# ScalarE's order in a softmax stage: the exponentials of one unit against the high half of another's probabilities

## The chip, the cores and the metric

One core of one Trainium2 chip runs the whole program. The metric is the device time of one execution in microseconds (us), as a median of several runs.

## What is computed

Two layers over 2048 tokens of width 1024. The first is sliding-window attention with 16 heads of 64 in 4 key/value groups and a sink per head; the second a pooling mixer. The change touches the attention's softmax. Cut from the reference:

```python
scores = jnp.einsum('bnqkgd,bnskd->bnkgqs', qb, kb).astype(jnp.float32) * (HEAD_DIM ** -0.5)
...
m = jnp.maximum(jnp.max(scores, axis=-1, keepdims=True), sink)
p = jnp.exp(scores - m)
denom = jnp.sum(p, axis=-1, keepdims=True) + jnp.exp(sink - m)
probs = (p / denom).astype(v.dtype)
o = jnp.einsum('bnkgqs,bnskd->bnqkgd', probs, vb)
...
return (o * jax.nn.silu(g)) @ w_out
```

## The kernel before

The program has four stages in a row on each engine: queries, keys and values (`qkv_stage`), gates (`gate_stage`), attention with its output projection (`attend_stage`), and the pooling layer (`pool_stage`). To keep float32 precision at the speed of the faster format, every operand of a large matmul is split into a high and a low half (ScalarE rounds to the high half, VectorE subtracts it from the value to get the low one), and three products are added up.

`attend_stage` works in 64 **units**: a unit is a block of 128 tokens by one key/value group, that is 4 heads. Nothing is scheduled by a tool: each engine has a hand-written loop over **slots** i = 0 to 67, and in slot i it does its piece of several units at once, in a fixed order. Engines wait for each other by semaphores, and each engine takes its instructions strictly in order. In slot i the pieces are:

- TensorE: scores of unit i (L1371); the first half of a weight fold (L1432) or of an output projection (L1415); the transposes of unit i-1's probabilities into the one buffer `tr` (L1381); the second half of fold or projection; the values of unit i-2 (L1399).
- ScalarE (`scalar`): the high half of z of unit i-3 (`z_hi`, L1207); the copy of the scores against the previous key block (`previous`, L1183); the high half of the transposed probabilities of unit i-1 (`p_hi`, L1198, into `ph`); the four exponentials of unit i with their sums (`exps`, L1191, into `pr` and `den`); in the first slots the high half of fold weights (`fold_high`, L1224 and L1227) and the eviction of a fold (`fold_evict`, L1232); in later slots, every second one, a square (L1214, L1217).
- VectorE (`vector`): the gating of unit i-3 (`gated`, L1289, into `z`); reciprocal and multiply of unit i-1 (`divide`, L1273, L1275); the predicated copy and maximum of unit i (`scores`, L1265, L1269); the low half of z (`z_lo`, L1296); every second slot a residual (L1304); the low half of unit i-1's probabilities (`p_lo`, L1281, into `pl`); in the first slots the low half of fold weights (`fold_low`, L1311 and L1313).
- GpSimd: four masks of unit i-1, two from `ph` and two from `pl`, into `pt` (L1147); every second slot the addition of a square (L1156).

A **fold** multiplies two weight matrices of the pooling layer ahead of time; there are 16, their weights are split in slots 0 to 15 and every fourth of these slots (0, 4, 8, 12) also splits a second weight. Output projections fill TensorE's slots from 19 on. The waits that matter here: `exps(u)` waits for the maximum of u (`max_done`), `p_hi(u)` for the transposes of u (`ptr_done`), `p_lo(u)` for `p_hi(u)` (`ph_done`), `previous(u)` for the scores (`s_done`), `z_hi(u)` for the gating (`z_done`), the transposes of u for the multiply of u (`prob_done`) and for `p_lo(u-1)` (`pl_done`), and the values of u for its four masks (`pt_done`).

Of the kernel before, what the change touches and what calls it, by code (L numbers as in the profile page):

```python
# [25 lines left out]
def wait(eng, sem, count):  # L26
    if count > 0:
        eng.wait_ge(sem, count)
# [931 lines left out]
def attend_stage(nc, sem_of, dims, weights, qk, ga, xt_d, sinks_d, wvt, w_group, qt_d, kt_d, vs_d, sg_d, wo_d, wp_d, x1t_d, ident,  # L960
# [8 lines left out]
    UNITS = NB * KV  # L969
# [56 lines left out]
    def chunks_ended(i):  # L1026
        return [c for c in range(CHUNKS - KC) if first_slot(c) + HALVES == i]

    def place(m):
        cur, prev = m % 3, (m - 1) % 3  # L1030
        return min(cur, prev), max(cur, prev), 0 if cur < prev else 1
# [141 lines left out]
    def scalar(act, next_hi):  # L1173
        def previous(u):
            m, g = u // KV, u % KV
            act.wait_ge(s_done, u + 1)
            wait(act, exp_done, u - 3)
            src = s_ps[:, u % 2, :, 1 - place(m)[2], :]
            if m == 0:
                act.wait_ge(consts_set, 5)  # L1180
                nc.scalar.activation(sc[:, g, :, 0:P], src, ACT.Identity, bias=first[:, :]).then_inc(prev_done, 1)
            else:
                nc.scalar.activation(sc[:, g, :, 0:P], src, ACT.Copy).then_inc(prev_done, 1)  # L1183

        def exps(u):
            g = u % KV
            act.wait_ge(max_done, u + 1)
            wait(act, ptr_done, u - 1)
            wait(act, rden_done, u - 1)
            for h in range(GROUP):  # L1190
                last = nc.scalar.activation(pr[:, u % 2, h, :], sc[:, g, h, :], ACT.Exp, bias=neg_max[:, u % 2, h:h + 1],  # L1191
                                            accum_out=den[:, u % 2, h:h + 1])
            last.then_inc(exp_done, 1)

        def p_hi(u):
            act.wait_ge(ptr_done, u + 1)
            wait(act, pt_done, 4 * u - 2)
            nc.scalar.activation(ph[:, :].bitcast(F32R), tr[:, :], ACT.Copy).then_inc(ph_done, 1)  # L1198

        def z_hi(u):  # L1200
            m, g = u // KV, u % KV
            s, t = m // PER, m % PER
            act.wait_ge(z_done, u + 1)
            wait(act, y_done, KC * (s - 1))
            if u == LAP:
                act.wait_ge(fold_done, FOLDS)
            nc.scalar.activation(zt[:, s % 2, HI, 2 * g:2 * g + 2, t * P:(t + 1) * P], z[:, u % 2], ACT.Copy).then_inc(zhi_done, 1)  # L1207

        def square(c):
            act.wait_ge(x1_done, c + 1)  # L1210
            s, d = c // KC, c % KC
            if d == 0:
                wait(act, st_done, s)
                nc.scalar.activation(acc[:, :], x_t[:, c % 3, :], ACT.Square).then_inc(sqx_done, 1)  # L1214
            else:
                wait(act, acc_done, (KC - 1) * s + (d - 2 if d >= 3 else 0))
                nc.scalar.activation(sqx[:, c % 2], x_t[:, c % 3, :], ACT.Square).then_inc(sqx_done, 1)  # L1217

        def fold_high(u):
            f = u // PAIRS  # L1220
            if u % PAIRS == 0:
                act.wait_ge(wg_loaded[f % 2], 16 * (f // 2 + 1))
                wait(act, fold_done, PAIRS * (f - 1))
                nc.scalar.activation(wg[:, f % 2, HI], wg_raw[:, f % 2], ACT.Copy).then_inc(wg_hi, 1)  # L1224
            act.wait_ge(fold_loaded[u % 3], 16 * (u // 3 + 1))
            wait(act, fold_done, u - 2)
            nc.scalar.activation(wv[:, u % 3, HI], wv_raw[:, u % 3], ACT.Copy).then_inc(fold_hi, 1)  # L1227

        def fold_evict(u):
            act.wait_ge(fold_done, u + 1)  # L1230
            wait(act, fold_stored[u % 2], 16 * GC * (u // 2))
            nc.scalar.activation(folded[:, u % 2].rearrange("p c k n -> p k c n"), fold_ps[:, u % 2], ACT.Copy).then_inc(fold_out, 1)  # L1232

        for i in range(LAST + 1):
            if 0 <= i - BEHIND < UNITS:
                z_hi(i - BEHIND)
            if i < UNITS:
                previous(i)
            if 1 <= i <= UNITS:
                p_hi(i - 1)  # L1240
            if i < UNITS:
                exps(i)
            if i < FOLDS:
                fold_high(i)
            if 0 <= i - 3 < FOLDS:
                fold_evict(i - 3)
            for c in chunks_ended(i):
                square(c)
        for c in range(CHUNKS - KC, CHUNKS):
            next_hi(act, c - CHUNKS + KC)  # L1250
            square(c)
# [219 lines left out]
    def last_rstd(pool):  # L1471
        rstd(pool, NSB - 1)

    return {"sync": sync, "gpsimd": gpsimd, "scalar": scalar, "vector": vector, "tensor": tensor, "first_load": first_load,
            "last_sum": last_sum, "last_mean": last_mean, "last_rstd": last_rstd, "chunks": CHUNKS, "units": UNITS, "s_done": s_done,
            "pt_done": pt_done, "o_done": o_done, "y_done": y_done, "ptr_done": ptr_done, "exp_done": exp_done, "cur_done": cur_done,
# [460 lines left out]
```

## Time and profile before

| | us |
|---|---|
| median of 3 runs | 1541.5 (1540.37 to 1541.74) |
| the profiled execution, its own time | 1541.43 |
| its span | 1539.7 |
| TensorE matmuls busy | 1438.1 (93% of the span) |
| VectorE busy | 895.0 (58%) |
| ScalarE busy | 542.1 (35%) |
| GpSimd busy | 385.7 (25%) |
| mean granted TensorE clock | 0.987 of full speed |

The span reaches from the first to the last recorded instruction; the time also holds what lies around it. A share is a mean over four stages: the stage of the change lies between 578.7 and about 946 us. In a timeline row the first number is the start from the span's start, the second the duration, and the brackets tell how long the engine idled just before and what ended the wait.

### The profile page before, as it was taken

The numbers are of one execution on the slowest core, as the hardware profiler recorded it, in microseconds if no ns is written. First come the engines' busy times: TensorE is split into PE (matmuls) and PEld (weight loads), VectorE is DVE, ScalarE is ACT, GpSimd is POOL, SyncE is SP. The second block draws the span as 40 slices with busy tenths as digits, with TensorE's granted clock in tenths as the row PEclk, the third lists the DMA queues.
The fourth block names the chain that finished last, engine by engine and source line by source line (L and its number), as shares of the span: only waits on it lengthen the run. The fifth ranks groups of instructions, "written<-read, shape, count | busy, mean of one in ns | idle before, by whom it ended". The sixth has DMA issues, their size and how long they took to land.

```text
span 1539.7 us, 20207 instructions
## 1 busy us (share of the span) xinstructions
PE 1438.1 (93%) x7240; PEld 1211.1 (79%) x7240; DVE 895.0 (58%) x1524; ACT 542.1 (35%) x1270; POOL 385.7 (25%) x551
## 2 busy tenths in 40 slices
PE   2789999999889996789999999899999999999999
PEld 1677777788678786778888888688888888888887
DVE  7766667665444446887777775535456452645522
ACT  2433334433211116775666564322222222222200
POOL 2333333321222213454555555220000000000000
PEclk9999999999989998999999999999999999999999
DMA  8644555534987786756767765941111552112142
GB/s 315 226 144 168 196 196 192 193 118 169 336 313 293 259 310 220 254 213 257 262 251 277 271 242 196 328 130 41 55 42 62 171 191 76 42 55 74 50 150 82
DMA packets 96787, 285.62 MB, mean 186 GB/s; under 512 B 10768, under 2 KB 40496, under 8 KB 87088
## 3 DMA queue, kind: packets, MB, share of 16 engines
q1 hardware_dynamic: 87760, 250.74, 45.3%
q0 software_dynamic: 8928, 33.59, 6.3%
q8 instruction: 58, 0.95, 0.2%
q14 instruction: 41, 0.34, 0.1%
HBM read 196.22 MB, written 88.08 MB: 185 GB/s over the span
## 4 chain that ended last, share of the span: by engine, by line
PE 58%; DMA 4%; DVE 4%; ACT 3%; issue 2%; POOL 0%; ACTq 0%; SPq 0%; DVEq 0%; POOLq 0%
PE po_f_ps L1843 23%; PE po_y_ps L1859 11%; PE at_y_ps L1415 9%; PE ga_g_ps L933 5%; PE at_o_ps L1399 5%; PE at_s_ps L1371 3%; PE at_tr L1381 2%; DMA ga_ada<-in_ada_w 2%; ACT at_pr L1191 1%; DMA x_mid_t<-at_x 1%; DMA po_xn<-x_mid_t 1%; DVE at_sc L1265 1%; DMA silu_gates_t<-ga_sg 1%; DVE at_neg_max L1269 1%; DVE at_z L1289 0%
## 5 line engine op out<-in xcount | busy, mean ns | idle before, releaser
L1843 PE MATMUL po_f_ps<-po_ht,po_w 128*128 128x512 f32 x1536 | 348.9, 389 | 0.0
L1843 PEld LDWEIGHTS po_f_ps<-po_ht,po_w 128*128 128x128 f32 x1536 | 288.1, 188 | 60.1 <-DVE po_ht L1705 0.3
L667 PE MATMUL qk_proj<-qk_w_qkv,qk_ht 128*128 128x512 f32 x1152 | 282.6, 401 | 12.7 <-DVE qk_ht L460 6.7
L667 PEld LDWEIGHTS qk_proj<-qk_w_qkv,qk_ht 128*128 128x128 f32 x1152 | 217.1, 192 | 59.9 <-DVE qk_ht L460 8.0
L1415 PE MATMUL at_y_ps<-at_zt,at_w 128*128 128x512 f32 x768 | 198.6, 400 | 5.8 <-DVE at_x L1304 5.2
L1859 PE MATMUL po_y_ps<-po_zt,po_w 128*128 128x512 f32 x768 | 174.7, 389 | 0.0
L1859 PEld LDWEIGHTS po_y_ps<-po_zt,po_w 128*128 128x128 f32 x768 | 144.1, 188 | 29.9
L1415 PEld LDWEIGHTS at_y_ps<-at_zt,at_w 128*128 128x128 f32 x768 | 138.4, 190 | 31.6 <-issue 7.1
L1692 DVE TENSOR_TENSOR po_w<-po_raw,po_w 128x1024 fp32r<-128x1024 f32 x48 | 58.8, 1225 | 129.1 <-ACT po_w L1626 129.1
L1147 POOL TENSOR_SCALAR_AFFINE_SELECT at_pt<-at_ph 128x512 fp32r<-128x512 f32 x128 | 83.6, 677 | 187.2 <-ACT at_ph L1198 187.2
L306 POOL TENSOR_TENSOR qk_rq<-qk_mq,qk_half 128x8 f32<-128x8 f32 (+1 forms) x48 | 70.2, 1462 | 189.4 <-DVE qk_mq L487 189.4
L1191 ACT ACTIVATE at_pr<-at_sc,at_neg_max 128x129 f32<-128x129 f32 x256 | 99.7, 393 | 7.2 <-DVE at_neg_max L1269 5.9
L1399 PE MATMUL at_o_ps<-at_pt,at_vs 128*128 128x256 f32 x744 | 100.6, 285 | 0.0
L1399 PEld LDWEIGHTS at_o_ps<-at_pt,at_vs 128*128 128x128 f32 x744 | 97.5, 192 | 3.8
L1626 ACT ACTIVATE po_w<-po_raw 128x1024 fp32r<-128x1024 f32 x48 | 50.6, 1054 | 108.4 <-PE po_y_ps L1859 108.4
L1551 POOL DMA_DIRECT2D po_xn<-x_mid_t x32 | 17.4, 544 | 262.7 <-DVE po_ht L1705 256.7
L1773 DVE SCALAR_TENSOR_TENSOR po_x<-po_y_ps,mod,po_x 128x512 f32<-128x512 f32 x32 | 24.0, 751 | 99.7 <-PE po_y_ps L1859 99.7
L1147 POOL TENSOR_SCALAR_AFFINE_SELECT at_pt<-at_pl 128x512 fp32r<-128x512 f32 x128 | 79.2, 641 | 3.2 <-DVE at_pl L1281 2.3
L1371 PE MATMUL at_s_ps<-at_kt,at_qt 128*128 128x256 f32 x512 | 73.0, 286 | 0.0
L872 ACT ACTIVATE ga_sg<-ga_g_ps 128x512 f32<-128x512 f32 x32 | 18.9, 595 | 142.7 <-PE ga_g_ps L933 113.9
L933 PE MATMUL ga_g_ps<-ga_x,ga_w_late 128*128 128x512 f32 x288 | 68.6, 398 | 0.0
L1371 PEld LDWEIGHTS at_s_ps<-at_kt,at_qt 128*128 128x128 f32 x512 | 67.3, 195 | 0.1
(168 smaller groups left out, 1985.8 us busy)
## 6 DMA issues: line engine op xcount, KB each, us to landing
at_w<-out_weight_split SPq DMA_DIRECT2D x32, 1024.0 KB, 6.6
queries_t<-qk_late SPq DMA_DIRECT2D x16, 1024.0 KB, 4.3
ga_ada<-in_ada_w POOLq DMA_DIRECT2D x64, 256.0 KB, 4.6
at_qt<-queries_t SPq DMA_DIRECT2D x16, 1024.0 KB, 8.2
ht_split<-qk_ht SPq DMA_DIRECT2D x6, 2048.0 KB, 9.6
values_split<-qk_late SPq DMA_DIRECT2D x16, 768.0 KB, 5.0
at_vs<-values_split SPq DMA_DIRECT2D x16, 768.0 KB, 5.0
qk_late<-in_ada_w SPq DMA_DIRECT2D x16, 512.0 KB, 5.6
```

The costliest lines, as they stand in the source:

```text
L306: nc.gpsimd.tensor_tensor(rq[:, heads], mq[:, heads], half[:, heads], ALU.pow).then_inc(rq_done, 1)
L667: last = nc.tensor.matmul(proj[:, b * BANK:(b + 1) * BANK], ht[:, s % 2, m, k, t * P:(t + 1) * P], w_qkv[:, w, k, b * BANK:(b + 1) * BANK] ...
L933: last = nc.tensor.matmul(g_bank(q), split_of(f, w)[:, k * P:(k + 1) * P], h, start=(i == 0), stop=(i == 3 * KC - 1))
L1147: nc.gpsimd.affine_select(out=pt[:, u % 2, kind, :].rearrange("p (h t) -> p h t", h=GROUP), in_=(ph if hi else pl)[:, :].rearrange("p (h t ...
L1191: last = nc.scalar.activation(pr[:, u % 2, h, :], sc[:, g, h, :], ACT.Exp, bias=neg_max[:, u % 2, h:h + 1], accum_out=den[:, u % 2, h:h + 1])
L1371: last = nc.tensor.matmul(s_ps[:, u % 2, h, :, :], qt[:, m % 2, GROUP * g + h, :], kt[:, low:high + 1:high - low, g, part, :], start=(part ...
L1399: last = nc.tensor.matmul(o_ps[:, 0:2 * P], v, moving[:, :, parity, :], start=(i == 0), stop=(i == 6 * len(parts) - 1))
L1415: last = nc.tensor.matmul(y_ps[:, c % 2, :], w[:, c % 3, a, k, :], zt[:, s % 2, b, k, :], start=(k == 0 and (a, b) == PRODUCTS[0]), stop=( ...
L1626: nc.scalar.activation(w[:, i % 2, HI].rearrange("p k c -> p (k c)"), raw[:, (RING0 + i) % RAW].rearrange("p k c -> p (k c)"), ACT.Copy).t ...
L1692: nc.vector.tensor_tensor(w[:, i % 2, LO].rearrange("p k c -> p (k c)"), raw[:, (RING0 + i) % RAW].rearrange("p k c -> p (k c)"), w[:, i % ...
L1843: last = nc.tensor.matmul(f_ps[:, bank(j, h), :], w[:, i % 2, a, k, :], ht[:, h, m, k, :], start=(n == 0), stop=(n == 3 * KC - 1))
L1859: last = nc.tensor.matmul(y_ps[:, h, :], w[:, i % 2, a, k, :], zt[:, h, m, k, :], start=(n == 0), stop=(n == 3 * KC - 1))
```

## The change

In each slot ScalarE takes `exps(i)` right after `previous(i)`, and `p_hi(i-1)` after it. No instruction, buffer or wait is added or removed; the other engines' programs are the same.

```diff
@@ -1236,10 +1236,9 @@
                 z_hi(i - BEHIND)
             if i < UNITS:
                 previous(i)
+                exps(i)
             if 1 <= i <= UNITS:
                 p_hi(i - 1)
-            if i < UNITS:
-                exps(i)
             if i < FOLDS:
                 fold_high(i)
             if 0 <= i - 3 < FOLDS:
```

ScalarE, one slot with a fold, before. L1207 is the high half of z, L1183 the copy of scores, L1198 the high half of the probabilities, L1191 the exponentials, L1227 the high half of the fold weights, L1232 the fold's eviction:

```order
L1207 ACTIVATE at_zt<-at_z 128x2x128
L1183 ACTIVATE at_sc<-at_s_ps 128x4x128
L1198 ACTIVATE at_ph<-at_tr 128x512
L1191 ACTIVATE at_pr,at_den<-at_sc,at_neg_max 128x129 x4
L1227 ACTIVATE at_early_wv<-at_early_wv_raw 128x512
L1232 ACTIVATE at_folded<-at_y_ps 128x2x2x128
```

The same slot with the change:

```order
L1207 ACTIVATE at_zt<-at_z 128x2x128
L1183 ACTIVATE at_sc<-at_s_ps 128x4x128
L1191 ACTIVATE at_pr,at_den<-at_sc,at_neg_max 128x129 x4
L1198 ACTIVATE at_ph<-at_tr 128x512
L1227 ACTIVATE at_early_wv<-at_early_wv_raw 128x512
L1232 ACTIVATE at_folded<-at_y_ps 128x2x2x128
```

The high half moves behind the four exponentials and stays ahead of the fold's two instructions. VectorE's order in such a slot is the same before and after; it ends with the low half of the probabilities (L1281) and of the fold weights (L1313), and the next slot begins with the gating (L1289):

```order
L1265 COPY_PREDICATED at_sc<-at_keep_cur,at_s_ps 128x4x128 [waits at_prev_done]
L1269 TENSOR_REDUCE at_neg_max<-at_sc 128x4 [waits at_exp_done,at_cur_done]
L1296 TENSOR_TENSOR at_zt<-at_z,at_zt 128x2x128 [waits at_zhi_done]
L1281 TENSOR_TENSOR at_pl<-at_tr,at_ph 128x512 [waits at_pt_done,at_ph_done]
L1313 TENSOR_TENSOR at_early_wv<-at_early_wv_raw,at_early_wv 128x512 [waits at_fold_hi]
L1289 SCALAR_TENSOR_TENSOR at_z<-at_o_ps,at_sg 128x256 [waits at_zlo_done,at_o_done]
L1273 RECIPROCAL at_rden<-at_den 128x4 [waits at_exp_done]
L1275 TENSOR_TENSOR at_pr<-at_pr,at_rden 128x4x128 [waits at_rden_done]
```

Nothing moved here; L1281 waits for the high half that now comes later.

## Rows read from the trace of the kernel before

**Rows 1.** The page, its first line.
```profile
span 1539.7 us, 20207 instructions
```

**Rows 2.** Windows: us, then busy us of each engine, TensorE clock, DMA share, GB/s.
```profile
602.00:680.00 78.00, 60.91 (x456) 56.24 (x456) 63.28 (x109) 54.95 (x172) 33.32 (x52) 0.98 0.69 241
609.00:613.50 4.50, 3.86 (x21) 3.66 (x20) 3.58 (x8) 2.93 (x11) 1.36 (x3) 0.62 0.91 310
680.00:689.00 9.00, 7.82 (x63) 7.24 (x61) 7.52 (x15) 7.11 (x25) 5.76 (x9) 1.00 0.74 280
770.00:860.00 90.00, 90.00 (x580) 79.96 (x578) 67.25 (x120) 55.03 (x184) 49.57 (x72) 1.00 0.69 259
```

**Rows 3.** Timeline of one fold slot: start us, us, engine, line, operation, idle before.
```profile
623.78 0.41 ACT L1191 ACTIVATE at_pr<-at_sc,at_neg_max 128x129 f32<-128x129 f32 x1 [0.31 <-DVE at_neg_max L1269]
...
625.34 0.62 ACT L1227 ACTIVATE at_early_wv<-at_early_wv_raw 128x512 fp32r<-128x512 f32 x1
...
625.99 0.89 DVE L1313 TENSOR_TENSOR at_early_wv<-at_early_wv_raw,at_early_wv 128x512 fp32r<-128x512 f32 x1 [0.94 <-ACT at_early_wv L1227]
...
626.80 0.41 DVE L1289 SCALAR_TENSOR_TENSOR at_z<-at_o_ps,at_sg 128x256 f32<-128x256 f32 x1
...
627.24 0.42 ACT L1207 ACTIVATE at_zt<-at_z 128x256 fp32r<-128x256 f32 x1 [0.81 <-DVE at_z L1289]
...
627.57 0.58 ACT L1183 ACTIVATE at_sc<-at_s_ps 128x512 f32<-128x512 f32 x1
...
628.18 0.74 DVE L1265 COPY_PREDICATED at_sc<-at_keep_cur,at_s_ps 128x512 f32<-128x512 uint32 x1 [0.16 <-ACT at_sc L1183]
...
628.95 0.69 DVE L1269 TENSOR_REDUCE at_neg_max<-at_sc 128x4 f32<-128x516 f32 x1
...
629.68 0.41 ACT L1191 ACTIVATE at_pr<-at_sc,at_neg_max 128x129 f32<-128x129 f32 x1 [0.31 <-DVE at_neg_max L1269]
```

**Rows 4.** Timeline, TensorE, the same slot.
```profile
626.58 0.94 PE L1432 MATMUL at_y_ps<-at_early_wg,at_early_wv 128*128 128x256 f32 x6 [0.64 <-ACT at_folded L1232]
628.08 0.66 PE L1381 MATMUL at_tr<-ident,at_pr 128*128 128x128 f32 x4 [0.56 <-DVE at_pr L1275]
```

**Rows 5.** Timeline, high half, low half, masks and gating in later slots.
```profile
687.29 0.68 DVE L1281 TENSOR_TENSOR at_pl<-at_tr,at_ph 128x512 f32<-128x512 f32 x1
...
687.89 0.41 DVE L1289 SCALAR_TENSOR_TENSOR at_z<-at_o_ps,at_sg 128x256 f32<-128x256 f32 x1
...
708.22 0.60 ACT L1198 ACTIVATE at_ph<-at_tr 128x512 fp32r<-128x512 f32 x1 [1.23 <-PE at_tr L1381]
...
708.85 0.69 DVE L1281 TENSOR_TENSOR at_pl<-at_tr,at_ph 128x512 f32<-128x512 f32 x1
708.88 1.22 POOL L1147 TENSOR_SCALAR_AFFINE_SELECT at_pt<-at_ph 128x512 fp32r<-128x512 f32 x2 [3.11 <-ACT at_ph L1198]
```

**Rows 6.** Timeline, ScalarE, first exponential of units 1, 16, 19 and 63.
```profile
588.37 0.39 ACT L1191 ACTIVATE at_pr<-at_sc,at_neg_max 128x129 f32<-128x129 f32 x1
...
678.11 0.41 ACT L1191 ACTIVATE at_pr<-at_sc,at_neg_max 128x129 f32<-128x129 f32 x1 [0.31 <-DVE at_neg_max L1269]
...
691.91 0.40 ACT L1191 ACTIVATE at_pr<-at_sc,at_neg_max 128x129 f32<-128x129 f32 x1
...
942.15 0.39 ACT L1191 ACTIVATE at_pr<-at_sc,at_neg_max 128x129 f32<-128x129 f32 x1
```

**Rows 7.** Timeline, TensorE, scores of two neighbouring slots with output projection.
```profile
705.23 1.12 PE L1371 MATMUL at_s_ps<-at_kt,at_qt 128*128 128x256 f32 x8
...
710.82 1.12 PE L1371 MATMUL at_s_ps<-at_kt,at_qt 128*128 128x256 f32 x8
```

**Rows 8.** Timeline, a GpSimd addition and the VectorE multiply beside it.
```profile
899.53 1.29 POOL L1156 TENSOR_TENSOR at_acc<-at_acc,at_sqx 128x512 f32<-128x512 f32 x1
...
899.77 1.60 DVE L1275 TENSOR_TENSOR at_pr<-at_pr,at_rden 128x512 f32<-128x512 f32 x1
```

**Rows 9.** Timeline, TensorE, the transposes of the last unit.
```profile
946.68 0.65 PE L1381 MATMUL at_tr<-ident,at_pr 128*128 128x128 f32 x4 [0.85 <-DVE at_pr L1275]
```

## Prediction

> **What bounds the kernel now.** The windows come first, because the change touches one stage only, from 578.7 to about 946 us of a span of 1539.7 us [rows 1], and that stage has three stretches with different limits. From 602 to 680 us TensorE is busy for 60.9 of 78.0 us, and no other engine is full either (VectorE 63.3, ScalarE 55.0, GpSimd 33.3): a stretch in which nobody is full is bounded by a loop of waits [rows 2]. From 680 to 689 us the slots have neither a weight fold nor an output projection. From 689 us on TensorE is busy all the time, 90.0 of 90.0 us between 770 and 860 [rows 2]: there TensorE sets the pace.
>
> The timeline of one slot of the first stretch shows the loop [rows 3]. From one unit's first exponential (623.78) it is 1.56 us until ScalarE is free for the high half of the fold weights (625.34), 0.65 until VectorE takes their low half (625.99), 0.81 until the gating behind it (626.80), 0.44 to the split of z on ScalarE (627.24), 0.33 to the copy of the previous scores (627.57), 0.61 to the predicated copy (628.18), 0.77 to the maximum (628.95) and 0.73 to the next unit's first exponential (629.68). The sum is 5.90 us, the whole slot. The high half of the probabilities, which the change moves, is on none of these steps. TensorE idles twice in that slot, 0.64 and 0.56 us [rows 4].
>
> In the third stretch two neighbouring slots begin 5.59 us apart (705.23 and 710.82) [rows 7]. Over all of it, from unit 19 (691.91) to unit 63 (942.15), 44 slots take 250.24 us, 5.69 each [rows 6].
>
> **The change, part by part.** No instruction is added or removed. Each of 64 high halves on ScalarE now stands behind four exponentials of the unit ahead, not before them. It can start no earlier than 1.56 us after the first exponential.
>
> *What is queued behind it.* VectorE's low half waits for the high half and starts 0.63 us after it (708.22 to 708.85) [rows 5]. Behind the low half, in VectorE's order, stand in a fold slot the low half of the fold weights, and then in every slot the next gating, which follows a low half after 0.60 us (687.29 to 687.89) [rows 5]. ScalarE's split of z waits for that gating, and behind the split stands the next copy of scores, which leads to the next exponentials. So a new loop is closed, one turn per slot: exponentials 1.56, high half to low half 0.63, low half to gating 0.60, then the known links 0.44 + 0.33 + 0.61 + 0.77 + 0.73. That is **5.67 us** in a slot without a fold. With a fold VectorE has one more operation of 0.60 between low half and gating, and the slot takes **6.27 us**. The second operand of that operation is no longer late: ScalarE makes it right behind the high half.
>
> *Fold slots, units 1 to 16.* 15 intervals, 89.74 us now (588.37 to 678.11) [rows 6]. Each grows by 6.27 - 5.90 = 0.37 at least. It can grow more, because the split of the fold weights now falls among GpSimd's masks, which start 0.66 us after the high half and run for 1.22 [rows 5]. What such a meeting costs is shown by a multiply that was asked for at 899.77 beside an addition on GpSimd running from 899.53 to 900.82: it ended at 901.37, 0.55 after the addition [rows 8]. The split would be asked for at 0.63 + 0.60 = 1.23 after the high half, at the joint between the first mask and the second (0.66 + 0.61 = 1.27). If it gets the joint it loses almost nothing, if not, about 0.5. I take 0.45 for the interval, near the lower end, since the margin is on its side: 15 x 0.45 = 6.8. Three of these slots begin a new weight group and have two splits in a row, the second certain to meet a mask: 3 x 0.4 = 1.2. Together **+8.0**; the ends are 15 x 0.37 = 5.6 and 15 x 0.9 = 13.5.
>
> A rule bears on this. The Trainium skill, "SBUF — State Buffer", Terms, says that VectorE and GpSimd take the port pair they share as an exclusive lock for a full instruction and that the loser blocks. The multiply above agrees. By that rule alone, with no look at the joint, every split would lose and the sum would be that of the first rival.
>
> *Units 16 to 19.* Three intervals take 13.80 us now (678.11 to 691.91) [rows 6]; at 5.67 each they take 17.0: **+3.2**. This is the surest term: TensorE has nothing here that would hide it.
>
> *Units 19 to 63.* The loop of 5.67 is longer than TensorE's 5.59, but the stretch now averages 5.69, since a part of its slots is lengthened, among others by meetings as in rows 8. 44 x 5.67 = 249.5 against 250.24: **-0.7**. TensorE cannot go under 44 x 5.59 = 246.0, which bounds a gain at 4.2; at 5.72 a slot the loss is 1.4.
>
> *Ends.* At unit 1 the exponentials no longer stand behind a high half: about -0.3. At unit 63, from the first exponential to the transposes it is 4.53 now (942.15 to 946.68) [rows 6, 9]; on the new path 1.56 + 0.63 + 0.60 and, from gating to transposes, 1.28 (626.80 to 628.08) [rows 3, 4], 4.07: **-0.5**. At a start of this size neither is more than a correction.
>
> *Costed at nothing.* GpSimd's four masks come later by the same 1.8 us as the high half, but TensorE needs them one slot later; in a slot with output projection about 1 us is left. The squares and fold evictions on ScalarE stand behind the high half too; they end 1.1 to 1.6 after it starts, and the gating's result is there only after 0.63 + 0.60 + 0.44 = 1.67. If that cover went, the split of z would wait for them. DMA issues stay in their order, on SP's queue. What comes after 946 us is bounded by TensorE and by data of this stage, so a delay passes through in full.
>
> The sum: 8.0 + 3.2 - 0.7 - 0.3 - 0.5 = **+9.7 us**. The profiled execution took 1541.43 us, its span 1539.7, and the median of the three runs is 1541.5, so both bases give the same: **1551.2 us**. About 0.2% (3 us) is what a measurement of this kernel can tell from no change.
>
> **The rivals.**
>
> *Lock lost at the joint.* The split of the fold weights comes a few hundredths later than 1.23 and finds the second mask running, to 1.88. Then it ends 0.55 after it, 0.5 later than assumed, in 15 slots: +7.5, **1558.7 us**. For it: a margin of 0.04 us. Against it: an operation already waiting when a mask ends should go first. If the multiply, asked for about 0.5 after the gating, loses its joint too (1.77 against the mask's end at 1.88), the predicated copy is some 0.4 later in the 44 slots as well: +17 more, 1576.
>
> *The idle time absorbs it (the other side).* ScalarE has 0.81 us idle before the split of z and VectorE 0.94 before the fold's low half [rows 3], more than the 0.50 and 0.60 that move there. If both moved operations fitted, first exponential to gating would stay 3.02 (623.78 to 626.80), the first two stretches would keep their times, and the third would run between 5.59 and 5.67: -0.7 to -4.2, about **1539 us**. It decides at 3.02: the new sequence is 1.56 + 0.63 + 0.60 + 0.60 = 3.39. It would need the low half not to hold up VectorE's next operation, and the in-order rows speak against that.
>
> *No effect.* The high half ends up at its old time because something else, already there, holds the exponentials as long: 1541.4. The 0.31 us idle ahead of the exponentials is a wait for the maximum [rows 3], so nothing of the kind is seen.
>
> *Clock.* Once in the first stretch, between 609.0 and 613.5 us, after a slot with two long waits, the granted clock was 0.62 of full speed [rows 2], a mix of the two levels of 1.2 and 2.4 GHz. Longer fold slots idle TensorE more. A drop of that length costs 0.38 x 4.5 = 1.7 us of work, against the slot's idle time of 0.64 + 0.56, which grows by 0.37: 0.1 us each, and perhaps 1 us where the third stretch starts. Five drops: about 1553. The Trainium skill, "TensorE: Matmul & The Clock Gate", Part 1, makes an idle engine fall to the half rate; by it the fold slots would fall oftener, and the time is this rival's.
>
> **How the numbers follow.** Forecast 0.64; lock lost 0.22 (0.04 of it in both places); no effect 0.06; absorbed 0.04; clock 0.04. The range holds the forecast's own bounds, 8.0 replaced by 5.6 and a third stretch at -2, to the lock lost with 2 us more: **1547 to 1561**. Left out are the two cases without a loss (0.10), the double loss (0.04) and a remainder. Slower 0.64 + 0.22 + 0.04 = 0.90, same 0.06, faster 0.04.
>
> **What would show it.** Fold slots near 6.3 us from first exponential to first exponential, 5.67 for units 16 to 19 and again near 5.7 from 19 to 63; the idle time before the fold's low half gone, and the low half of the probabilities directly before it; TensorE idle before the transposes in the third stretch, by under 0.1 us a slot. A fold's low half of 1.1 us or more would be the first rival. Wrong I would be if the fold slots stayed at 5.9, or if the third stretch left 5.6 to 5.75.

## The result, and the profile after

| | before | with the change |
|---|---|---|
| median | 1541.62 us (4 runs, 1540.37 to 1542.31) | 1555.06 us (4 runs, 1553.16 to 1556.96) |
| ratio | | 1.0089, 95% interval 1.0077 to 1.0102 |
| the profiled execution, its own time | 1541.43 | 1556.96 |
| mean granted TensorE clock | 0.987 | 0.981 |

The change costs 13.4 us. It was forecast to cost 9.7, within 1547 to 1561.

The first line of the page after stands against [rows 1]; the profiled execution was the slowest of its four, so its span is 15.5 us longer, 2 more than the medians differ.

```profile
span 1555.2 us, 20207 instructions
```

To see where the 15.5 us are, the first exponential of each unit is read from the ScalarE timeline of both kernels. The intervals between them add up to this (positions in us from the span's start; units 1, 16, 19 and 63 of before are [rows 6]):

| stretch | before | after | difference | forecast |
|---|---|---|---|---|
| start of the program to unit 0 | 582.36 | 583.16 | +0.8 | 0 |
| unit 0 to 1 | 6.01 | 5.72 | -0.3 | -0.3 |
| units 1 to 16 (fold slots) | 89.74 | 100.10 | +10.4 | +8.0 |
| units 16 to 19 | 13.80 | 17.01 | +3.2 | +3.2 |
| units 19 to 63 | 250.24 | 251.37 | +1.1 | -0.7 |
| unit 63 to the end of the span | 597.55 | 597.84 | +0.3 | -0.5 |

The windows after, with the same columns as [rows 2]:

```profile
602.00:690.00 88.00, 64.72 (x455) 60.35 (x454) 62.48 (x107) 54.38 (x175) 43.92 (x52) 0.92 0.62 211
690.00:700.00 10.00, 6.92 (x53) 6.13 (x52) 6.53 (x13) 6.02 (x20) 5.77 (x8) 0.97 0.74 274
700.00:860.00 160.00, 159.71 (x1015) 142.00 (x1016) 115.73 (x212) 92.57 (x323) 94.94 (x124) 0.99 0.68 255
```

TensorE is still busy nearly all the time in the last of them (159.71 of 160.00), but it gets less done: 1015 matmuls, against 1025 in the same window of the kernel before. In that kernel VectorE's gating waited for TensorE's values in 42 of the 44 slots recorded between 700 and 945 us; in the changed kernel only the two slots that hold the sums of squares wait for them. The stretch is no longer TensorE's: one slot there shows the ring of the prediction, link by link. The timeline of ScalarE and VectorE, units 22 and 23:

```profile
723.03 0.40 ACT L1191 ACTIVATE at_pr<-at_sc,at_neg_max 128x129 f32<-128x129 f32 x1 [1.55 <-DVE at_neg_max L1268]
...
724.59 0.58 ACT L1198 ACTIVATE at_ph<-at_tr 128x512 fp32r<-128x512 f32 x1
...
725.20 0.69 DVE L1280 TENSOR_TENSOR at_pl<-at_tr,at_ph 128x512 f32<-128x512 f32 x1 [1.87 <-ACT at_ph L1198]
...
725.81 0.41 DVE L1288 SCALAR_TENSOR_TENSOR at_z<-at_o_ps,at_sg 128x256 f32<-128x256 f32 x1
...
726.25 0.42 ACT L1207 ACTIVATE at_zt<-at_z 128x256 fp32r<-128x256 f32 x1 [1.09 <-DVE at_z L1288]
...
726.58 0.58 ACT L1183 ACTIVATE at_sc<-at_s_ps 128x512 f32<-128x512 f32 x1
...
727.19 0.75 DVE L1264 COPY_PREDICATED at_sc<-at_keep_cur,at_s_ps 128x512 f32<-128x512 uint32 x1 [0.16 <-ACT at_sc L1183]
...
727.97 0.69 DVE L1268 TENSOR_REDUCE at_neg_max<-at_sc 128x4 f32<-128x516 f32 x1
...
728.70 0.41 ACT L1191 ACTIVATE at_pr<-at_sc,at_neg_max 128x129 f32<-128x129 f32 x1 [1.54 <-DVE at_neg_max L1268]
```

First exponential 723.03, high half 724.59 (+1.56), low half 725.20 (+0.61), gating 725.81 (+0.61), split of z 726.25 (+0.44), copy 726.58 (+0.33), predicated copy 727.19 (+0.61), maximum 727.97 (+0.78), next first exponential 728.70 (+0.73): 5.67 us. Of the 44 intervals from unit 19 to 63, 42 lie between 5.66 and 5.70. Before, they alternated between about 5.43 and 5.88 in most of the stretch, and VectorE's multiply met GpSimd's addition of a square, as in [rows 8], in 18 of the 43 slots between 697 and 940 us (1.59 to 1.62 us instead of 0.69). In the changed kernel 42 of the 43 multiplies take 0.69: the masks come later, the addition stands behind them, and so it no longer runs beside the multiply. The change thus closes a ring in this stretch and takes meetings out of it, and the two nearly cancel. The exponentials now wait for the maximum (1.54 us in the slot shown), and VectorE's low half waits for the high half; the same operation had no such wait in [rows 5].

A fold slot after, which stands against [rows 3]:

```profile
623.40 0.58 ACT L1198 ACTIVATE at_ph<-at_tr 128x512 fp32r<-128x512 f32 x1
...
624.01 0.69 DVE L1280 TENSOR_TENSOR at_pl<-at_tr,at_ph 128x512 f32<-128x512 f32 x1 [1.87 <-ACT at_ph L1198]
...
624.04 1.75 POOL L1147 TENSOR_SCALAR_AFFINE_SELECT at_pt<-at_ph 128x512 fp32r<-128x512 f32 x2 [3.12 <-ACT at_ph L1198]
...
624.62 0.68 DVE L1312 TENSOR_TENSOR at_early_wv<-at_early_wv_raw,at_early_wv 128x512 fp32r<-128x512 f32 x1
...
625.22 0.42 DVE L1288 SCALAR_TENSOR_TENSOR at_z<-at_o_ps,at_sg 128x256 f32<-128x256 f32 x1
...
625.67 0.42 ACT L1207 ACTIVATE at_zt<-at_z 128x256 fp32r<-128x256 f32 x1 [0.69 <-DVE at_z L1288]
...
625.75 1.18 DVE L1274 TENSOR_TENSOR at_pr<-at_pr,at_rden 128x512 f32<-128x512 f32 x1
...
625.75 1.67 POOL L1147 TENSOR_SCALAR_AFFINE_SELECT at_pt<-at_pl 128x512 fp32r<-128x512 f32 x2
...
626.85 0.74 DVE L1264 COPY_PREDICATED at_sc<-at_keep_cur,at_s_ps 128x512 f32<-128x512 uint32 x1
...
628.35 0.41 ACT L1191 ACTIVATE at_pr<-at_sc,at_neg_max 128x129 f32<-128x129 f32 x1 [1.78 <-DVE at_neg_max L1268]
```

Two things are to be seen here. The split of the fold weights on VectorE (624.62) got its turn at the joint of two masks, as forecast: it took 0.68 us, no more. But GpSimd paid for it. Its first pair of masks, 1.22 us in [rows 5], takes 1.75 here and ends at 625.79, and VectorE's multiply is asked for at 625.75, just as a mask of the next pair takes over. The multiply lasts 1.18 us. The predicated copy, which follows in VectorE's order, starts at 626.85, 1.63 behind the gating instead of 1.38 in [rows 3]. So the slot, from the first exponential at 621.84 to the next at 628.35, takes 6.51 us and not 6.27. In the three slots with a new weight group the second split takes 1.12 us instead of 0.68 besides, and they take 7.54.

### The profile page after: what moved, and what is told of

Its sections match the earlier page's. It is cut to its first block, busy times and chain, and to the rows that moved or that the text cites. A ratio compares the mean times of both kernels' runs of the same rounds, so it can differ in the third digit from the quotient of the medians.

```text
span 1555.2 us, 20207 instructions
## 1 busy us (share of the span) xinstructions
PE 1444.4 (93%) x7240; PEld 1217.1 (78%) x7240; DVE 891.7 (57%) x1524; ACT 533.8 (34%) x1270; POOL 415.8 (27%) x551
## 4 chain that ended last, share of the span: by engine, by line
PE 56%; DVE 12%; issue 10%; DMA 8%; ACT 7%; POOL 6%; SPq 1%; POOLq 0%; ACTq 0%; DVEq 0%
PE po_f_ps L1842 22%; PE po_y_ps L1858 11%; PE qk_proj L667 9%; PE ga_g_ps L933 6%; POOL at_pt L1147 3%; PE at_y_ps L1414 3%; DMA ga_ada<-in_ada_w 3%; ACT at_pr L1191 3%; DMA po_xn<-x_mid_t 1%; PE at_o_ps L1398 1%; DVE at_sc L1264 1%; DVE at_neg_max L1268 1%; POOL at_acc L1156 1%; DMA ga_raw<-in_attn_w_gate 1%; POOL qk_rq L306 1%
## 5 line engine op out<-in xcount | busy, mean ns | idle before, releaser
L1191 ACT ACTIVATE at_pr<-at_sc,at_neg_max 128x129 f32<-128x129 f32 x256 | 100.0, 392 | 104.3 <-DVE at_neg_max L1268 104.3
L1147 POOL TENSOR_SCALAR_AFFINE_SELECT at_pt<-at_pl 128x512 fp32r<-128x512 f32 x128 | 107.8, 864 | 0.0
L1398 PEld LDWEIGHTS at_o_ps<-at_pt,at_vs 128*128 128x128 f32 x744 | 101.9, 201 | 4.5 <-issue 0.7
L1398 PE MATMUL at_o_ps<-at_pt,at_vs 128*128 128x256 f32 x744 | 104.9, 292 | 0.5 <-issue 0.5
L1280 DVE TENSOR_TENSOR at_pl<-at_tr,at_ph 128x512 f32<-128x512 f32 x64 | 44.3, 692 | 92.8 <-ACT at_ph L1198 92.8
```

The lines of the kernel that those rows point to most:

```text
L1147: nc.gpsimd.affine_select(out=pt[:, u % 2, kind, :].rearrange("p (h t) -> p h t", h=GROUP), in_=(ph if hi else pl)[:, :].rearrange("p (h t ...
L1398: last = nc.tensor.matmul(o_ps[:, 0:2 * P], v, moving[:, :, parity, :], start=(i == 0), stop=(i == 6 * len(parts) - 1))
```

## The experiments

Two theories stand against each other. **The ring**: the delayed high half closes a loop through the in-order queues of ScalarE and VectorE, and its price in a stretch is the loop's length less what bounded the stretch before. **A price per slot**: each of 64 high halves is late, and everything behind it is late by the same 0.21 us. Beside them, for the fold slots, the port of VectorE and GpSimd against TensorE's clock.

### The change in some slots only

The changed order in slots 16 to 63 alone, shown against the changed kernel:

```diff
             if i < UNITS:
                 previous(i)
+            if FOLDS <= i < UNITS:
                 exps(i)
             if 1 <= i <= UNITS:
                 p_hi(i - 1)
             if i < FOLDS:
+                exps(i)
+            if i < FOLDS:
                 fold_high(i)
```

> The changed order only in slots 16 to 63; in slots 0 to 15 the high half stands ahead of the exponentials as in the kernel before. Theory of the loop (the delay is that of the closed ring high half, low half, gating, copy, maximum, exponentials, and its price depends on what else stands on that ring): units 1 to 16 back to 89.7 us from first exponential to first exponential, 16 to 19 at 17.0, 19 to 63 at 251.4; that is 4.3 us more than the kernel before, 1546 us. Rival, a price per slot whatever stands in it (64 delayed high halves, 13.4 us, 0.21 each): 48 of 64 slots, 10 us more, 1552.

Measured: 1544.77 us, ratio to the kernel before 1.0026 (1.0014 to 1.0037), which is 4.0 us more. Units 1 to 16 took 90.3, 16 to 19 17.00, 19 to 63 251.5.

The other half, with the changed order in slots 0 to 15 and the old one from 16 on, again against the changed kernel:

```diff
             if i < UNITS:
                 previous(i)
+            if i < FOLDS:
                 exps(i)
             if 1 <= i <= UNITS:
                 p_hi(i - 1)
+            if FOLDS <= i < UNITS:
+                exps(i)
```

> The changed order only in slots 0 to 15. Theory of the loop: units 1 to 16 take 100.1 us as in the changed kernel (ordinary intervals 6.51, those of a new weight group 7.54), 16 to 19 13.8 and 19 to 63 250.2 as in the kernel before: 10.4 - 0.3 = 10.1 more, 1551.7 us. Rival, a price per slot: 16 of 64 slots, 3.4 more, 1545. Added to the other half's loss the two should give the whole loss of 13.4, if nothing is shared between the stretches.

Measured: 1551.9 us, ratio 1.0066 (1.0053 to 1.0078), 10.2 more. Units 1 to 16 took 100.04, 16 to 19 13.93, 19 to 63 250.21. A quarter of the slots carries three quarters of the loss; a price per slot would have put 3.4 us here and 10 in the other half. The two parts make 14.2, the whole 13.7 by its ratio. Each of these figures is uncertain by about 2 us, so no sharing between the stretches is to be seen, and the intervals in the traces agree: each stretch is as in the kernel whose order it has, within 0.6 us.

### A link taken out of the ring

In the changed kernel ScalarE copies the previous scores first and splits z after that, so the copy no longer waits for the gating:

```diff
         for i in range(LAST + 1):
+            if i < UNITS:
+                previous(i)
             if 0 <= i - BEHIND < UNITS:
                 z_hi(i - BEHIND)
             if i < UNITS:
-                previous(i)
                 exps(i)
```

> The changed kernel, with ScalarE's copy of the previous scores ahead of the split of z, so that the copy no longer waits for the gating. Theory of the loop: the predicated copy then waits for the multiply alone, 0.54 + 0.60 = 1.14 behind the gating instead of 1.39: units 16 to 19 5.42 each, 16.3 instead of 17.0; 19 to 63 bounded by TensorE again, 5.59 to 5.65 a slot, 246.5 to 249 instead of 251.4; the fold slots unchanged at 6.51, since there the multiply is already what the predicated copy waits for. Total 1550 to 1552. Rival, the split of z is not on the ring (ScalarE is simply late by the moved order): no interval changes, 1555.

Measured: 1550.4 us, ratio 1.0060 (1.0048 to 1.0073). Units 16 to 19 took 5.42, 5.42 and 5.41, 16.25 in all; 19 to 63 took 248.1; units 1 to 16 99.9. All as the ring has it: the fold slots did not move, as said, and the other two stretches did. A slot between 16 and 19, ScalarE and VectorE:

```profile
692.09 0.58 ACT L1183 ACTIVATE at_sc<-at_s_ps 128x512 f32<-128x512 f32 x1
...
692.35 0.41 DVE L1289 SCALAR_TENSOR_TENSOR at_z<-at_o_ps,at_sg 128x256 f32<-128x256 f32 x1
...
692.80 0.42 ACT L1207 ACTIVATE at_zt<-at_z 128x256 fp32r<-128x256 f32 x1
...
692.88 0.69 DVE L1275 TENSOR_TENSOR at_pr<-at_pr,at_rden 128x512 f32<-128x512 f32 x1
...
693.49 0.74 DVE L1265 COPY_PREDICATED at_sc<-at_keep_cur,at_s_ps 128x512 f32<-128x512 uint32 x1
```

The copy (692.09) stands ahead of the gating (692.35), and the predicated copy follows the multiply at once: 693.49 - 692.35 = 1.14. The split of z is on the ring only because the copy stood behind it.

A second cut, at another link of the changed kernel: VectorE's low half of units 16 to 63 goes behind the next slot's gating.

```diff
             if 0 <= i - BEHIND < UNITS:
                 gated(i - BEHIND)
+            if FOLDS <= i - 2 < UNITS:
+                p_lo(i - 2)
             if 1 <= i <= UNITS:
                 divide(i - 1)
...
-            if 1 <= i <= UNITS:
+            if 1 <= i <= FOLDS:
                 p_lo(i - 1)
```

> The changed kernel, with VectorE's low half of units 16 to 63 moved from the end of its slot to behind the next slot's gating, so that the gating no longer waits for the high half. Theory of the loop: the link low half to gating (0.60) is gone from the ring, and the rest gives 0.63 + 0.61 + 0.20 + 0.60 + 0.77 + 0.73 + 1.56 = 5.1 a turn, or 5.6 if the multiply now meets a mask: units 16 to 19 15.5 to 16.8 instead of 17.0, 19 to 63 TensorE's own 246 to 250 instead of 251.4; units 1 to 16 unchanged at 100.1. Total 1550 to 1554. Rival, the low half is late as such (masks and values late, TensorE waits for them): with the low half later still, 16 to 63 get longer, above 268.4 in all.

Measured: 1558.22 us, ratio 1.0115 (1.0100 to 1.0130). Units 16 to 63 took 270.7 us together: the total is above the ring's range, and the stretch is where the rival put it, above 268.4. By these numbers the rival came true, so the trace has to tell which of the two is at work.

Units 16 to 19 took 16.43, two of the three intervals 5.38. That is the ring with a link cut out: exponentials 1.56, then 0.60 to the low half, 0.61 to the reciprocal, 0.21 to the multiply, 0.91 to the predicated copy, 0.76 to the maximum and 0.73 to the next exponentials. The 0.91 would be 0.61 without a mask: the multiply takes 0.99 us here instead of 0.69.

But 19 to 63 took 254.2: the intervals alternate between 5.40 and 6.03. The larger part of the difference is a meeting at the port, in every second slot. VectorE and GpSimd in two neighbouring slots:

```profile
723.77 0.42 DVE L1288 SCALAR_TENSOR_TENSOR at_z<-at_o_ps,at_sg 128x256 f32<-128x256 f32 x1 [1.84 <-PE at_o_ps L1400]
...
724.91 0.69 DVE L1274 TENSOR_TENSOR at_pr<-at_pr,at_rden 128x512 f32<-128x512 f32 x1
...
725.00 1.68 POOL L1147 TENSOR_SCALAR_AFFINE_SELECT at_pt<-at_pl 128x512 fp32r<-128x512 f32 x2
...
729.36 0.42 DVE L1288 SCALAR_TENSOR_TENSOR at_z<-at_o_ps,at_sg 128x256 f32<-128x256 f32 x1 [1.38 <-PE at_o_ps L1400]
...
730.45 1.67 POOL L1147 TENSOR_SCALAR_AFFINE_SELECT at_pt<-at_pl 128x512 fp32r<-128x512 f32 x2
...
730.50 1.13 DVE L1274 TENSOR_TENSOR at_pr<-at_pr,at_rden 128x512 f32<-128x512 f32 x1
```

At 724.91 the multiply is asked for 0.09 ahead of the masks and takes 0.69; at 730.50 it comes 0.05 behind them and takes 1.13. The expectation had this meeting in its 5.6 for a turn, but not that the masks and the multiply would start within 0.1 us of each other in every slot. The meeting makes 0.44 of the 0.63 us between the two kinds of slot. The other 0.19 lies ahead of the gating, which now waits for TensorE's values (the brackets at 723.77 and 729.36) and starts 2.15 us after the first exponential in one slot and 2.34 in the next; why it alternates was not tested. The rival's mechanism, TensorE waiting for late masks, is not seen: from 706 to 940 us the trace has no wait of TensorE for a mask. So the run bears out the ring for units 16 to 19. In the last stretch it puts another limit in the ring's place, and does not show what the ring alone would cost there.

### The port in the fold slots

The changed kernel; the masks of units 0 to 15 wait for one thing more, the multiply of the next unit:

```diff
             hi = kind in (CUR_HI, PREV_HI)
+            if u < FOLDS and kind == CUR_HI:
+                pool.wait_ge(prob_done, u + 2)
             pool.wait_ge(ph_done if hi else pl_done, u + 1)
```

> The changed kernel, and GpSimd's masks of units 0 to 15 wait besides for the multiply of the next unit, so that they no longer run while VectorE multiplies. Theory of the port (6.51 instead of 6.27 because the multiply meets a mask and ends late, 1.18 us instead of 0.69, and the second split of a weight group likewise): multiply back to 0.69 us, ordinary intervals 6.27, those of a weight group 6.87, units 1 to 16 about 95 us instead of 100.1, total about 1550 us. Rival, the interval is 6.51 for another reason (the clock of TensorE, which is lower in this stretch than before): no change or, as a wait is added, slower, 1555 or more.

Measured: 1550.89 us, ratio 1.0063 (1.0049 to 1.0076): a wait was added, and the kernel is about 4 us faster than the changed one. VectorE's multiply in the fold slots (a row has busy us, mean ns of one, idle us before): first the kernel before, then the changed kernel, then this one.

```profile
L1275 DVE TENSOR_TENSOR at_pr<-at_pr,at_rden 128x512 f32<-128x512 f32 x13 | 9.0, 692 | 0.5
```

```profile
L1274 DVE TENSOR_TENSOR at_pr<-at_pr,at_rden 128x512 f32<-128x512 f32 x12 | 14.1, 1175 | 0.4
```

```profile
L1276 DVE TENSOR_TENSOR at_pr<-at_pr,at_rden 128x512 f32<-128x512 f32 x12 | 8.3, 692 | 0.4
```

692, 1175, 692 ns. The ordinary intervals are 6.26 and 6.27, those of a weight group 6.87, which are the lengths expected without a meeting. That settles the port: in the changed kernel it costs 6.51 - 6.27 = 0.24 in an ordinary fold slot and 7.54 - 6.87 = 0.67 in one with a new weight group. Units 1 to 16 took 97.5, not 95: two intervals were 7.37 and 7.39. Ahead of each, TensorE's values wait for the later masks and then run slowly; here is the second (the window row has the columns of [rows 2]):

```profile
651.75 2.61 PE L1400 MATMUL at_o_ps<-at_pt,at_vs 128*128 128x256 f32 x11 [1.27 <-POOL at_pt L1149]
...
645.00:655.00 10.00, 7.98 (x51) 7.40 (x51) 6.04 (x12) 6.61 (x22) 2.58 (x4) 0.84 0.21 63
```

Twelve of these matmuls take 1.6 us elsewhere at full clock; eleven took 2.61 here, in a window in which the granted clock was 0.84 of full speed, a mix of its two levels of 2.4 and 1.2 GHz (0.50 from 652 to 655 us). Before them TensorE idled 1.27 us; it idled as long at 631.24 too, the clock stayed at full speed, and that interval is not long. The scores behind the slow matmuls were late and held up the copy by 0.45 us. The clock rival is thus real where TensorE has no slack left, and absent in the changed kernel, whose clock from 602 to 690 us was 0.92 and whose ordinary intervals were 6.49 to 6.52 all the same.

### A shorter ring for the kernel before

If the fold slots of the kernel before are bound by a ring, it can be shortened. The diff is against the kernel before; its fold pieces on ScalarE move to where ScalarE waits for the maximum:

```diff
             if i < UNITS:
                 previous(i)
-            if 1 <= i <= UNITS:
-                p_hi(i - 1)
-            if i < UNITS:
-                exps(i)
             if i < FOLDS:
                 fold_high(i)
             if 0 <= i - 3 < FOLDS:
                 fold_evict(i - 3)
+            if 1 <= i <= UNITS:
+                p_hi(i - 1)
+            if i < UNITS:
+                exps(i)
```

> The kernel before, with the fold's pieces on ScalarE (high half of the fold weights, eviction) put ahead of the high half of the probabilities and the exponentials, where ScalarE waits for the maximum anyway. If the price of a fold slot is what stands on the ring exponentials, fold's high half, fold's low half, gating, copy, maximum (5.90), then taking the fold off it leaves what the slots without a fold show, 4.5, or TensorE's own work in such a slot, 5.90 - 0.64 - 0.56 = 4.7: units 1 to 16 in 70 to 74 us instead of 89.7, total 1522 to 1530. Rival, the fold slots are bounded by the loads of the fold weights or by the port of VectorE and GpSimd: 85 us or more, 1537 or more.

Measured: 1524.67 us (1517.8 to 1528.14), ratio 0.9886 (0.9865 to 0.9907): 17.6 us less than the kernel before by the ratio, 15.6 by the medians. Units 1 to 16 took 76.7 instead of 89.7, less gain than the 70 to 74 expected. These rows say why:

```profile
624.69 0.62 ACT L1227 ACTIVATE at_early_wv<-at_early_wv_raw 128x512 fp32r<-128x512 f32 x1
...
625.21 0.59 ACT L1232 ACTIVATE at_folded<-at_y_ps 128x512 f32<-128x512 f32 x1
...
625.90 0.60 ACT L1198 ACTIVATE at_ph<-at_tr 128x512 fp32r<-128x512 f32 x1
...
626.57 0.41 ACT L1191 ACTIVATE at_pr<-at_sc,at_neg_max 128x129 f32<-128x129 f32 x1
...
627.38 1.10 DVE L1313 TENSOR_TENSOR at_early_wv<-at_early_wv_raw,at_early_wv 128x512 fp32r<-128x512 f32 x1
...
628.41 0.41 DVE L1289 SCALAR_TENSOR_TENSOR at_z<-at_o_ps,at_sg 128x256 f32<-128x256 f32 x1
...
632.01 0.60 ACT L1232 ACTIVATE at_folded<-at_y_ps 128x512 f32<-128x512 f32 x1 [1.74 <-DMA value_weight_folded<-at_folded]
```

The fold's high half (624.69) now stands ahead of the exponentials (626.57), as meant. The fold's low half (627.38) no longer waits for it, but takes 1.10 beside masks, and the slot is 4.96. And one eviction, at 632.01, waited 1.74 us for the store of an earlier fold, with the high half and the exponentials behind it: that interval is 6.41. So the lengths of 5.9 before were the ring's. With the ring gone, the operations beside masks are the long ones in an ordinary slot, and one slot is held by a store.

With the last stretch changed as well (from slot 19 on: copy, split of z, exponentials, high half), shown against the kernel just told of:

```diff
+            late = i >= FOLDS + BEHIND
+            if late and i < UNITS:
+                previous(i)
             if 0 <= i - BEHIND < UNITS:
                 z_hi(i - BEHIND)
-            if i < UNITS:
+            if not late:
                 previous(i)
...
+            if late and i < UNITS:
+                exps(i)
             if 1 <= i <= UNITS:
                 p_hi(i - 1)
-            if i < UNITS:
+            if not late:
                 exps(i)
```

> The same, and from slot 19 on the order of the changed kernel with the copy of scores ahead of the split of z, which in that stretch took 248.1 us against 250.2 before. If the gains add up: 2 us less than with the fold's pieces moved alone. Rival: the 2 us were the multiply meeting GpSimd's additions at a phase that depends on how the stretch is entered, and the two kernels are equal.

Measured: 1521.23 us, ratio 0.9879 (0.9861 to 0.9898). By the intervals of the ratios the two kernels can't be told apart; by the trace units 19 to 63 took 247.9 against 250.3, the expected 2 us, with 5.58 to 5.61 in all but three slots. Where the kernel just told of still has 19 of the 41 multiplies between 697 and 940 us at 1.59 us or more, here 39 of 41 take 0.69. Units 1 to 16, where the two programs are the same, took 75.3 against 76.7: the wait for the store, 1.74 us there, was 0.89 here, so its length varies between executions.

Last, in this kernel the first mask of the low half of units 0 to 15 waits for the next multiply, and the second stands behind it:

```diff
             hi = kind in (CUR_HI, PREV_HI)
+            if u < FOLDS and kind == CUR_LO:
+                pool.wait_ge(prob_done, u + 2)
             pool.wait_ge(ph_done if hi else pl_done, u + 1)
```

> The previous experiment's kernel (fold's pieces ahead; copy first and exponentials first from slot 19 on), in which a fold slot takes 4.97 us and its multiply 1.17 beside a mask. Here the two masks of the low half, for units 0 to 15, wait besides for the next unit's multiply. Theory of the port: the multiply back to 0.69 and the ordinary fold slots to TensorE's own 4.7, since some 0.3 of the 0.48 shows before TensorE sets the pace: units 1 to 16 in 71 to 73 us instead of 75.3, total about 1518. Rival: the values now wait for the later masks, TensorE is held up, and the slots are as long or longer, 75 or more, 1521 or more.

Measured: 1520.12 us, ratio 0.9859 (0.9837 to 0.9881). The ordinary fold slots are 4.74 instead of 4.97, the multiply 0.69; units 1 to 16 took 74.1, with one interval of 6.82 that holds a wait of 2.13 us for a store. Both 74.1 and the total lie between what the theory and the rival expected. The gain over the kernel ahead of it is 1.2 us in these units and within the uncertainty of the ratios. Its median is the lowest of the kernels tried, 1.4% below the kernel before by the ratio.

## Why the prediction was right, and where it was short

**The ring, 5.67 us a turn: right.** The sum of links from rows of the kernel before came out to the hundredth, in the changed kernel from unit 16 on and in the half with the new order from 16. That the last digit agrees is luck: three links were off by 0.01 or 0.02 and cancel.

**Units 16 to 19, +3.2: right**, measured +3.2, and back to 13.9 where only the fold slots had the new order.

**Fold slots, +8.0: too little by 2.4.** The term that failed is the 0.45 for an interval, of which 0.37 is the ring and 0.08 was meant for the port. The ring's 6.27 was confirmed when the masks were moved away. The port costs 0.24 in an ordinary slot and 0.67 in one with a second split, where 0.08 and 0.48 were allowed. The second split was priced right, 0.4 against 1.12 - 0.68 = 0.44; what was missing is the multiply, in all 15 intervals. The price of a meeting, about 0.5 from [rows 8], was right too. The error was to look at one meeting only. I asked whether the split would get the joint between two masks; it did, by a few hundredths as worked out. I did not follow what GpSimd does then: its masks move back, the pair by 0.53 us. In an undisturbed row the third mask would have ended at about 624.04 + 1.22 + 0.61 = 625.87, an estimate, only 0.12 us after the multiply is asked for; now it begins at 625.75, and the multiply waits for all of it. The later masks were costed at nothing with TensorE in view, and for TensorE that was right: from 588 to 690 us it has no wait for a mask. VectorE paid. It is not the rival "lock lost at the joint", in which the split itself would have been long (0.68 measured), but its neighbour, with about half its price, since the predicated copy waits for the copy of scores as well and only 0.25 of the multiply's 0.49 comes through.

**Units 19 to 63, -0.7: wrong in sign, by 1.9.** 42 intervals were as forecast. The other two, 6.41 and 6.56, hold the sums of squares, 8 small matmuls that TensorE fits in once per 16 slots. I used the stretch's mean for before, which has them, and a bare 44 x 5.67 for after, which has not. In the changed kernel they show at 0.7 and 0.9. Both wait for GpSimd's addition, which stands behind the masks and so comes later too; in the kernel before the same matmuls have no such wait. The second of them, with the values behind it and what VectorE does then:

```profile
894.76 1.05 PE L1353 MATMUL at_o_ps<-at_ones,at_acc 128*128 128x1 f32 x8 [0.29 <-POOL at_acc L1156]
895.68 1.68 PE L1398 MATMUL at_o_ps<-at_pt,at_vs 128*128 128x256 f32 x12
...
897.48 0.42 DVE L1288 SCALAR_TENSOR_TENSOR at_z<-at_o_ps,at_sg 128x256 f32<-128x256 f32 x1
...
898.02 1.19 DVE L1274 TENSOR_TENSOR at_pr<-at_pr,at_rden 128x512 f32<-128x512 f32 x1
```

The values end at 897.36 and the gating has to wait for them: it starts 1.25 us after the low half (896.23), not 0.61. The rest of the 0.9 is the port, with the multiply at 1.19. The same place with the copy taken off the ring still had 6.55, where the slots around it are bound by TensorE at 5.6. That the ring would absorb TensorE's extra 0.8 us was an assumption without a row.

The comparison of 5.67 with 5.69 hides a second thing. The 5.69 of before is not TensorE's pace alone. A pair of slots with a meeting takes about 11.31 us instead of 2 x 5.59 = 11.18, so 18 pairs make some 2.3 us by this estimate; from 250.3 to 247.9 is what came off in the kernel that in this stretch has neither the ring nor the meetings with the addition.

**Ends.** Start of the ring -0.3, as said. The -0.5 at unit 63 came where it was worked out: from its first exponential (957.36) to the transposes it is 4.06 us, with 4.07 forecast and 4.53 before. The row stands against [rows 9]:

```profile
961.42 0.66 PE L1380 MATMUL at_tr<-ident,at_pr 128*128 128x128 f32 x4 [0.82 <-DVE at_pr L1274]
```

It doesn't show in the table, because the rest of the program, from these transposes to the end of the span, took 593.8 us instead of 593.0. Up to the pooling layer's first matmuls both take 10.2 us of it, so what was lost was lost in the pooling layer. Its program is the same, and its time varies: in the profiles of the six kernels that are alike from the transposes on, the rest took 591.7 to 595.2 us. So does the part ahead of the stage, with its +0.8: in the profiles of the seven kernels that are alike up to there, the first exponential of unit 0 came between 578.5 and 583.2 us.

**The other cases.** "No effect" and "absorbed" fell with the first interval table: the idle 0.81 and 0.94 us of [rows 3] were waits inside the ring, not room. The clock fell more often, 0.92 from 602 to 690 us against 0.98 before, and cost nothing there that the intervals show: the ordinary slots are 6.49 to 6.52, the ring's and the port's length.

## What to carry to other kernels

In hand-ordered queues, moving one instruction behind another on one engine can close a loop through the in-order neighbours: write down who waits for it, what stands behind the waiter, and follow that until you are back; the length of the loop against the stretch's present slot is the price. It is different for each stretch, so count slots by kind. And idle time inside such a loop is no room to move work into: on the kernel before, taking a piece off the loop gained about 16 to 18 us, where the change, which puts another piece on a loop, cost 13.4. Last, a new order on one engine moves the meetings of the engines behind it: count those that it makes and those that it takes away.

## What the runs showed of the hardware

- Which of VectorE and GpSimd waits can be a matter of 0.14 us. With the later low half, the same multiply took 0.69 when asked for 0.09 us ahead of a mask and 1.13 when asked for 0.05 behind its start. In the changed kernel the loss repeats in all 12 fold slots of the row shown (mean 1175 ns): it is a phase that the program's order fixes, not noise.
- In every meeting looked at, the VectorE operation ended about 0.55 us after the GpSimd instruction that it met, whether that was a mask of 0.61 (1.13 to 1.18 us in all) or an addition of 1.29 (1.60, [rows 8]).
- A split that wins the joint lengthens GpSimd's pair of masks from 1.22 to 1.75 us, and so moves the meeting to the next VectorE operation. The Trainium skill, "SBUF — State Buffer", Who interferes with whom, says that issue order, not the shape of the operation, decides who blocks; the rows of the multiply and the masks shown of the kernel with the later low half agree with it.
- An added wait on GpSimd made the changed kernel about 4 us faster (1.0063 against 1.0089 of the kernel before), since it moved masks out of the multiply's way (692 ns against 1175).
